# An encoder trunk on one core: order of the norm transitions and of the cross attention's head norms

## The reference, cut to what matters

```
h = rms_norm(x, mix_norm[l])
x = x + mixer(h) @ w_out          # layer 0: RWKV-7 and a gating MLP; layer 1: differential attention
# cross attention, 4 heads of 256, into 256 memory tokens
q = rms_norm((rms_norm(x, cross_norm[l]) @ wq).reshape(.., 4, 256), q_gain)
kv = rms_norm(mem, mem_norm) @ wkv
k = rms_norm(kv[..., :1024].reshape(.., 4, 256), k_gain);  v = kv[..., 1024:]
x = x + (softmax(q k^T / 16) v) @ wo
# gated MLP, width 2816
u = conv3(rms_norm(x, ffn_norm[l]) @ w_up)
x = x + (silu(gate) * val) @ w_down
```

## Time and profile before

| | |
|---|---|
| median of 3 runs | 1874.19 us (1871.98 to 1876.8) |
| the profiled execution's own time | 1874.89 us |
| its span, first to last instruction | 1873.1 us |
| PE busy with matmuls | 1759.9 us, 94% of the span |
| DVE, ACT, POOL busy | 989.2, 766.8, 100.6 us |
| mean granted TensorE clock | 0.984 of full speed |

### The profile page before, as it was taken

One profiled execution on the slowest core, in us unless ns is written; L12 is line 12 of the kernel. 1 busy time (PEld: TensorE's weight loads), 2 busy tenths in 40 slices (PEclk: granted clock), 3 DMA queues, 4 the chain that ended last, 5 costly groups with the idle time before them and its releaser, 6 DMA issues.

```text
span 1873.1 us, 31962 instructions
## 1 busy us (share of the span) xinstructions
PE 1759.9 (94%) x14153; PEld 1442.8 (77%) x14153; DVE 989.2 (53%) x1353; ACT 766.8 (41%) x1158; POOL 100.6 (5%) x79
## 2 busy tenths in 40 slices
PE   6997888889999999999998999999998999999999
PEld 5876777767778788888887887557777878888887
DVE  5477656467434456534644244994534356633652
ACT  4243444334644334413433234773554244422431
POOL 1001221000000000000000022000000000000000
PEclk9999999989999999999998999999999999999999
DMA  7210000033331222233212322002322213322221
GB/s 237 79 45 2 4 4 4 5 136 122 135 112 45 68 90 91 99 103 111 92 68 90 112 78 80 1 1 91 134 68 91 83 60 105 110 93 90 90 83 75
DMA packets 96452, 149.40 MB, mean 80 GB/s; under 512 B 3479, under 2 KB 50170, under 8 KB 96314
## 3 DMA queue, kind: packets, MB, share of 16 engines
q1 hardware_dynamic: 94727, 142.29, 22.6%
q0 software_dynamic: 1296, 4.95, 0.8%
q10 hardware_dynamic: 291, 0.12, 0.0%
HBM read 145.25 MB, written 2.10 MB: 79 GB/s over the span
## 4 chain that ended last, share of the span: by engine, by line
PE 79%; DVE 11%; ACT 5%; issue 3%; DMA 2%; POOL 1%; POOLq 0%; DVEq 0%; SPq 0%; ACTq 0%
PE PS L373 65%; DVE SS L1560 1%; PE PS L506 1%; PE PS L956 1%; DVE WLO L338 1%; ACT WHI L330 1%; PE PS L1349 1%; PE PS L1318 1%; PE PS L942 1%; PE PS L983 1%; PE PS L975 1%; PE PS L588 1%; DMA WRAW<-cross_wo 1%; DMA WRAW<-cross_wq 1%; DVE YQ L1287 1%
## 5 line engine op out<-in xcount | busy, mean ns | idle before, releaser
L338 DVE TENSOR_TENSOR WLO<-WRAW,WHI 128x2048 fp32r<-128x2048 f32 (+1 forms) x132 | 296.7, 2251 | 458.3 <-ACT WHI L330 458.3
L330 ACT ACTIVATE WHI<-WRAW 128x2048 fp32r<-128x2048 f32 (+1 forms) x132 | 248.1, 1880 | 471.1 <-PE PS L373 442.6
L373 PE MATMUL PS<-HIS,WHI 128*128 128x512 f32 x856 | 333.8, 390 | 1.5 <-DVE SM L1722 1.5
L373 PE MATMUL PS<-HIS,WLO 128*128 128x512 f32 x856 | 333.0, 389 | 0.0
L373 PE MATMUL PS<-LOS,WHI 128*128 128x512 f32 x856 | 333.0, 389 | 0.0
L373 PE MATMUL PS<-WHI,HIS 128*128 128x512 f32 x608 | 239.1, 393 | 7.3 <-DVE WLO L338 3.5
L373 PE MATMUL PS<-WLO,HIS 128*128 128x512 f32 x608 | 237.4, 391 | 0.0
L373 PE MATMUL PS<-WHI,LOS 128*128 128x512 f32 x608 | 237.3, 390 | 0.0
L373 PEld LDWEIGHTS PS<-HIS,WHI 128*128 128x128 f32 x856 | 160.7, 188 | 35.0 <-DVE SM L1722 1.7
L373 PEld LDWEIGHTS PS<-HIS,WLO 128*128 128x128 f32 x856 | 160.7, 188 | 33.6
L373 PEld LDWEIGHTS PS<-LOS,WHI 128*128 128x128 f32 x856 | 160.7, 188 | 33.4 <-issue 0.2
(11 more groups left out here) (280 smaller groups left out, 2467.1 us busy)
## 6 DMA issues: line engine op xcount, KB each, us to landing
WRAW<-ffn_w_up SPq DMA_DIRECT2D x88, 512.0 KB, 4.6
WRAW<-ffn_w_down SPq DMA_DIRECT2D x20, 1024.0 KB, 5.0
WRAW<-cross_wkv SPq DMA_DIRECT2D x16, 1024.0 KB, 5.0
WRAW<-diff_w_in SPq DMA_DIRECT2D x12, 1024.0 KB, 5.0
WRAW<-ab_w_in SPq DMA_DIRECT2D x10, 1024.0 KB, 5.3
WRAW<-cross_wq SPq DMA_DIRECT2D x8, 1024.0 KB, 5.0
WRAW<-cross_wo SPq DMA_DIRECT2D x8, 1024.0 KB, 5.1
X<-x SPq DMA_DIRECT2D x8, 512.0 KB, 7.2
```

The lines of the kernel that those rows point to most:

```text
L330: A.e.activation(part(WHI[i % 3], i), part(WRAW[i % 2], i), ACT.Copy).then_inc(S("w_hi"), 1)
L338: V.e.tensor_tensor(part(WLO[i % 3], i), part(WRAW[i % 2], i), part(WHI[i % 3], i).bitcast(F32), ALU.subtract).then_inc(S("w_lo"), 1)
L373: mm = e.matmul(o, l, r, start=(si == 0 and kk == 0 and q == 0), stop=(si == len(steps) - 1 and kk == nk - 1 and q == 2))
```

## The change

- A product whose operand comes from a norm waits for each block k before that block's first matmul, in tile b = 0, instead of for four blocks ahead of the slab.
- The squares of the three tile-wise norm transitions are taken by half rows: the first half's squares (and their DVE step, with the epsilon) stand in the evacuation of the first column half; the second half's squares are 512 wide, and the mean-square instruction adds the first half's.
- `norm_pe` for n1 uses all eight banks and does not wait from k = 4 on.
- kk's second column half uses banks 2 and 3 instead of 0 and 1. The bank waits are kept per bank instead of per base.
- Head norms go tile by tile: DVE's mean squares (4 columns), POOL's power (4 columns) and DVE's scaling stand in the evacuation of the second column half, the scaling one tile behind.
- The query transposes stand ahead of the tiles of slab kv1 instead of kv2 on PE, and ACT's evacuation of them ahead of its split of slab kv1 + 2 = kv3, by a new argument `ahead`.

```diff
@@ gemm_pe
-            if operand is not None and gi == 0:
-                e.wait_ge(*operand(kb + nk))
...
-                if si == 0 and banks_before[name, gi] is not None:
+                if si == 0 and banks_before[name, gi, b] is not None:
...
                     k = kb + kk
+                    if operand is not None and gi == 0 and b == 0:
+                        e.wait_ge(*operand(k + 1))
@@ gemm_side
             for i, _, _ in steps:
+                if ahead is not None:
+                    ahead(s)
                 split(E, i + 3 if limit is None else min(i + 3, limit))
@@ bank_base
+        if name.startswith("kk") and gi == 1:
+            return 2
@@ square_tile_act
-            if gi == 1:
-                A.e.wait_ge(*at(name, "ev", n + 1))
-                if b > 0:
-                    A.e.wait_ge(*at(tag, "sq", b))
-                A.e.activation(SQ[:, :], X[:, b, :], ACT.Square, accum_out=SM[:, b:b + 1]).then_inc(sem(tag, "sq"), 1)
+            half = slice(gi * 512, gi * 512 + 512)
+            A.e.wait_ge(*at(name, "ev", n + 1))
+            if n > 0:
+                A.e.wait_ge(*at(tag, "sq", n))
+            o = (12, 0)[gi] + b
+            A.e.activation(SQ[:, half], X[:, b, half], ACT.Square, accum_out=SM[:, o:o + 1]).then_inc(sem(tag, "sq"), 1)
@@ var_tile_dve and residual_and_norm_dve
+    def half_var_dve(V, tag, t):
+        V.e.wait_ge(*at(tag, "sq", t + 1))
+        V.mine(V.e.tensor_scalar(SM[:, 12 + t:13 + t], SM[:, 12 + t:13 + t], 1.0 / D, EPS, ALU.mult, ALU.add))
...
-        V.e.wait_ge(*at(tag, "sq", t + 1))
-        V.e.tensor_scalar(SM[:, 4 + t:5 + t], SM[:, t:t + 1], 1.0 / D, EPS, ALU.mult, ALU.add).then_inc(sem(tag, "var"), 1)
+        V.e.wait_ge(*at(tag, "sq", NT + t + 1))
+        V.e.tensor_scalar(SM[:, 4 + t:5 + t], SM[:, t:t + 1], 1.0 / D, SM[:, 12 + t:13 + t], ALU.mult, ALU.add)\
+            .then_inc(sem(tag, "var"), 1)
...
+            if gi == 0:
+                if b >= 1:
+                    half_var_dve(V, tag, b - 1)
+                if b == NT - 1:
+                    half_var_dve(V, tag, b)
+                    V.wait_mine()
@@ norm_pe
-            if k >= 4:
+            if k >= 4 and b0 is not None:
@@ head_norm_dve
-        V.e.wait_ge(*at(name, "ev", gemms[name][-1][2] + gemms[name][-1][1]))
-        group_var_dve(V, tag, nt, XD, 32 + o, 96 + o)
+        def evac(gi, b, banks):
+            if gi == 1:
+                e.wait_ge(*at(name, "ev", banks + 1))
+                s = 32 + o + b * n
+                e.tensor_scalar(SM[:, s + 64:s + 64 + n], SM[:, s:s + n], 1.0 / XD, EPS, ALU.mult, ALU.add)\
+                    .then_inc(sem(tag, "gvar"), 1)
+                if b > 0:
+                    scale(b - 1)
+                if b == nt - 1:
+                    scale(b)
@@ head_norm_pool
         for t in range(nt):
-            group_scale_dve(V, tag, tok, t, XD, 160 + o)
+            G.e.wait_ge(*at(tag, "gvar", t + 1))
+            s = 96 + o + t * n
+            G.e.tensor_tensor(SM[:, s + 64:s + 64 + n], SM[:, s:s + n], SM[:, 16:17].to_broadcast([P, n]), ALU.pow)\
+                .then_inc(sem(tag, "grstd"), 1)
@@ query_turn_pe
-            if (gi, si) == (1, 0):
+            if (gi, si) == (0, 1):
+                if b == 0:
+                    T.e.wait_ge(*at(f"xq{l}", "ev", 2 * NT))
@@ tensor_program and scalar_program
-                norm_pe(T, "n1", XN, NT, 4)
+                norm_pe(T, "n1", XN, NT, None)
...
             def query_turn(s):
-                if s == 2:
+                if s == 1:
...
-            gemm_side(A, f"kv{l}", split_hi, copy_out(A, f"kv{l}", to_tok(VMEM)), only=0)
-            gemm_side(A, f"kv{l}", split_hi, None, beside=query_turn, only=1)
+            gemm_side(A, f"kv{l}", split_hi, copy_out(A, f"kv{l}", to_tok(VMEM)), ahead=query_turn, only=0)
+            gemm_side(A, f"kv{l}", split_hi, None, only=1)
```

More of the change, by code:

```diff
@@ L378, in gemm_pe, with gemm_side @@
                 mm.then_inc(sem(name, "wused"), 1)
-    def gemm_side(E, name, split, evac, limit=None, beside=None, only=None):
+    def gemm_side(E, name, split, evac, limit=None, beside=None, only=None, ahead=None):
         s = 0
@@ L403, in bank_base, with norm_bank @@
             return 6
+        if name.startswith("kk") and gi == 1:
+            return 2
         return 4 if name.startswith("dn") or (name, gi) == ("ab", 1) else 0
-    banks_before, before = {}, {0: None, 4: None, 6: None}
+    banks_before, before = {}, [None] * 8
     for _name, _groups in gemms.items():
         for _gi, (_, _nb, _banks) in enumerate(_groups):
-            banks_before[_name, _gi] = before[bank_base(_name, _gi)]
-            before[bank_base(_name, _gi)] = (_name, _nb, _banks)
+            for _b in range(_nb):
+                _bank = bank_base(_name, _gi) + _b
+                banks_before[_name, _gi, _b] = before[_bank]
+                before[_bank] = (_name, _banks + _b + 1)
     def bank_free(name, gi, b):
-        other, nb, banks = banks_before[name, gi]
-        return at(other, "ev", banks + min(b, nb - 1) + 1)
+        other, n = banks_before[name, gi, b]
+        return at(other, "ev", n)
     hhi, hlo = (lambda k: HHI[k][:, :]), (lambda k: HLO[k][:, :])
+    def norm_bank(b0, k):
+        return k if b0 is None else b0 + k % 4
     def norm_act_front(A, tag, src, sq, nt, arrives=False, added=None):
@@ L435, in norm_act_back @@
             e.wait_ge(*at(tag, "tp", k + 1))
-            e.activation(hi(k)[:, 0:nt * P], PS[:, b0 + k % 4, 0:nt * P], ACT.Copy,
+            e.activation(hi(k)[:, 0:nt * P], PS[:, norm_bank(b0, k), 0:nt * P], ACT.Copy,
                          scale=gain(k)).then_inc(sem(tag, "hi"), 1)
@@ L454, in norm_dve_back @@
             e.wait_ge(*at(tag, "hi", k + 1))
-            e.scalar_tensor_tensor(lo(k)[:, 0:nt * P], PS[:, b0 + k % 4, 0:nt * P], gain(k),
+            e.scalar_tensor_tensor(lo(k)[:, 0:nt * P], PS[:, norm_bank(b0, k), 0:nt * P], gain(k),
                                    hi(k)[:, 0:nt * P].bitcast(F32), ALU.mult, ALU.subtract).then_inc(sem(tag, "lo"), 1)
@@ L486, in evac @@
             add(gi, b, n)
-            if gi == 1:
+            if gi == 0:
[4 more added lines that the diff above has]
+                    V.wait_mine()
+            else:
                 if b >= 1:
@@ L505, in norm_pe @@
                     e.wait_ge(*at(tag, "xn", t + 1))
-                mm = e.transpose(PS[:, b0 + k % 4, t * P:t * P + P], xn[:, t, k * P:k * P + P], ident)
+                mm = e.transpose(PS[:, norm_bank(b0, k), t * P:t * P + P], xn[:, t, k * P:k * P + P], ident)
             mm.then_inc(sem(tag, "tp"), 1)
@@ L559, in evac @@
             for q in range(2):
-                A.e.activation(SQX[:, 0:XD], PS[:, b, q * XD:q * XD + XD], ACT.Square,
+                A.e.activation(SQX[:, 0:XD], PS[:, bank_base(name, gi) + b, q * XD:q * XD + XD], ACT.Square,
                                accum_out=SM[:, sums + 4 * b + 2 * gi + q:sums + 4 * b + 2 * gi + q + 1])\
@@ L563, in evac, with scale, head_norm_pool @@
                 A.e.wait_ge(*at(name, "hsum", 2 * n + q + 1))
-            A.e.activation(dst(gi, b), PS[:, b, :], ACT.Copy).then_inc(sem(name, "ev"), 1)
+            A.e.activation(dst(gi, b), PS[:, bank_base(name, gi) + b, :], ACT.Copy).then_inc(sem(name, "ev"), 1)
         return evac
     def head_norm_dve(V, tag, name, tok, nt, o):
-        V.e.wait_ge(*at(name, "ev", gemms[name][-1][2] + gemms[name][-1][1]))
-        group_var_dve(V, tag, nt, XD, 32 + o, 96 + o)
+        e, n = V.e, D // XD
+        def scale(t):
+            e.wait_ge(*at(tag, "grstd", t + 1))
+            v = tok[:, t, :].rearrange("p (g w) -> p g w", w=XD)
+            e.tensor_tensor(v, v, SM[:, 160 + o + t * n:160 + o + t * n + n].unsqueeze(2).to_broadcast([P, n, XD]), ALU.mult)\
+                .then_inc(sem(tag, "gn"), 1)
+        def evac(gi, b, banks):
[8 more added lines that the diff above has]
+                    scale(b)
+        return evac
+    def head_norm_pool(G, tag, nt, o):
+        n = D // XD
         for t in range(nt):
-            group_scale_dve(V, tag, tok, t, XD, 160 + o)
+            G.e.wait_ge(*at(tag, "gvar", t + 1))
+            s = 96 + o + t * n
+            G.e.tensor_tensor(SM[:, s + 64:s + 64 + n], SM[:, s:s + n], SM[:, 16:17].to_broadcast([P, n]), ALU.pow)\
+                .then_inc(sem(tag, "grstd"), 1)
     def group_norm_pool(G, tag, nt, w, o=0):
@@ L1748, in norm_shares @@
         n = nt if by_tile else 1
-        shares(tag, "norm", sq=nt, var=n, rstd=n, xn=nt, tp=DC, hi=DC, lo=DC)
+        shares(tag, "norm", sq=2 * nt if by_tile else nt, var=n, rstd=n, xn=nt, tp=DC, hi=DC, lo=DC)
     def turn_shares(tag, nt):
-        n = DH if tag == "do" else 1
+        n = DH if tag == "do" else nt if tag[0] == "x" else 1
         shares(tag, "turn", gvar=n, grstd=n, gn=DH if tag == "do" else nt, ttp=DC, tev=DC, hi=DC if tag == "do" else 0)
@@ L1958, in vector_program @@
             if l == 1:
```

(8 more changed lines are left out.)

4 lines of the change are left out of this document (2 added, 2 removed).

## The result

The changed kernel takes 1856.82 us (median of 4, 1856.34 to 1859.2); the kernel before, with one more run beside it, 1873.62 us. The ratio is 0.9905, 95% interval 0.9892 to 0.9917: 16.8 us less, where 17.0 was forecast. The profiled execution took 1856.78 us, 18.1 less than the one of before.

What follows compares the result with a forecast made beforehand. PE carries 79% of the chain, so time is won at its waits. Terms 3.2 + 11.8 + 2.0 = 17.0 us take the profiled 1874.9 to 1857.9; that execution lay 0.7 above the median, so 1857.2 us, range 1852 to 1865.

Steps and rivals of the forecast that it cites:

- Keys and banks: Start of xq: PE no longer waits for ACT's evacuation of the keys; 1.6 us in each layer, 3.2 us.
- Queries: Cross attention, kv's first product to first logits: 25.7 us falls to 19.8, 5.9 in each layer, 11.8 us.
- the slack of 0.15: Cross attention: the queries' last scaling ends 0.15 us before PE turns to their transposes ahead of kv1.
- What is late next: Softmax weights behind ACT's later kv3 split: ready 1.3 us before PE needs them, so nothing lost; the tightest place.
- Rival 1: Softmax starts late: load, splits or evacuations take 3 to 4 us more, PE waits 2 to 3 per layer; 1862, 16%.
- Squares: Norm transitions, squares by half rows: 0.4 us each at nf0 and nf1, 1.2 at n1, together 2.0 us.
- Eight banks and waits for each k: Norm transitions: no gain, as PE's transposes are slow at half clock; at full clock n1 would win about 1.1 us.
- rival 2: Norm transitions' idle gaps: clock staying up gives up to 7 us more, 1850; staying down longer, 1861; 17%.
- Rivals 3 and 4: Nothing comes of the query part, 1869, 4%; or slower, as ACT's late kv3 split delays the softmax weights, 1879, 3%.

Runs made afterwards that it cites:

- e1: Kernel before with only kk's second half in banks 2 and 3 and bank waits kept per bank; 1867.97 us, ratio 0.9970.
- e2: Kernel before with only the query part: head norms tile by tile and query transposes at slab kv1; 1861.04 us, ratio 0.9933.
- e5: Kernel before with only the query transposes moved to slab kv1, head norms in one piece; 1874.32 us, ratio 1.0001.
- e6: Kernel before with only the head norms tile by tile, query transposes at kv2 as before; 1863.04 us, ratio 0.9938.
- e7: Changed kernel with four unused 1024-wide squares on ACT between query evacuation and kv3's split in each layer; 1869.52 us in one execution.
- e4: Kernel before with only the waits for each k and the eight banks of n1; 1872.33 us, ratio 0.9995.
- e11: Changed kernel with spare products on PE in the norm transitions' gaps, but n1 back on four banks; 1854.86 us, ratio 0.9897.
- e9: Changed kernel with spare products on PE in the gaps of the three norm transitions; 1851.39 us, ratio 0.9882.
- e12: As e10, but products wait once for each slab of four blocks, as in the kernel before; 1854.45 us, ratio 0.9885.
- e3: Kernel before with only the squares by half rows; 1870.15 us, ratio 0.9981.
- e8: Changed kernel with each tile's scaling directly behind its own power, so none runs beside a power; 1859.20 us in one execution.
- e10: As e9, with eight banks at nf0 and nf1 too; 1849.82 us, ratio 0.9870.

## Why the prediction was right

- **Keys and banks: 3.2 forecast, 3.5 in the trace of the change, 3.75 alone (e1).** The mechanism is as worked out; the term was read from the wait's row, 1.6 in each layer. A row's idle time begins where the last product's row ends, and a row is 0.39 us long where products follow every 0.227. A wait that goes away therefore gives back 0.16 more than its row says, and 1.58 + 0.16 = 1.74 is what e1 shows (1.77 and 1.75). The changed kernel has 1.69 and 1.55, for its nx transposes waited 0.28 and 0.36 for a low half, where the kernel before waited 0.21 and 0.17.
- **Queries: 11.8 forecast, 11.8 measured, 11.8 alone by e2's stages (12.1 by its medians).** 19.8 us of work were forecast between kv's first product and the logits, 19.88 are there. The power beside a scaling was taken at 2.0 and took 1.91; the slack of 0.15 was 0.10. What the forecast did not say is which half of the change brings it: e5 and e6 show that it is the norm tile by tile, through DVE's earlier split of kv2 and the earlier load of xo0. The move of the turn alone does nothing (e5), and on top of the norm it gives 0.2 in each layer.
- **What is late next: slack 1.3 forecast, 0.9 measured.** The first exponential was forecast 7.7 us after the logits (22.0 - 14.3) and came after 8.04. e7 bears the 0.9 out. Rival 1 named the right place; its condition, 3 to 4 us more than was counted, did not occur.
- **Squares: 2.0 forecast.** The gaps ahead of the last tile shrank by 0.47, 0.47 and, at n1, 1.28 (from 7.16 to 5.88 us after the last product): 2.2.
- **Eight banks and waits for each k: nothing forecast, nothing measured (e4).** The condition was the right one: at n1 the gain was put at 1.1 us if the clock were up, and e11 against e9 gives 1.13. Its make-up was not seen. The prediction says that the first slab's low halves have been waited for by the time the last transpose is issued. That holds with four banks only; with eight, and the clock up, the waits for each k carry 0.8 of the 1.13 (e12).
- **The clock, rival 2.** It was down in all three transitions, as forecast, but not for as long: 0.8 us of the 18.1 come from the lengths from the last tile's transposes to the first product (nf0 5.67 to 5.01, nf1 5.02 to 4.81, n1 5.81 to 5.90). The sum has no term for that. Nothing in the change itself makes the work of nf0 and nf1 shorter; the clock came back a little earlier, and whether the shorter gap brings that about is not shown (in e3, with the same gap, nf1 went the other way, to 5.79).
- **How much of the match is luck.** The profiled executions differ by 18.1, 1.1 over the forecast: 0.8 of the clock, 0.3 of the keys and 0.2 of the squares, less the 0.2 lost ahead of them. The medians differ by 16.8. A match to 0.2 us is closer than either can tell, with runs that spread over 2.9 and 4.8 us; the mechanism is borne out by the stages, not by that match.
- **Rivals 3 and 4** did not occur. 3 needed the queries' last tile to be late, and 0.1 us was left. e5 is its case, with the last scaling 4 us late, and there nothing came of the query part.

The power beside a 1.22 us scaling with two SBUF inputs took 1.91, and in e8, with nothing beside it, 1.01. The Trainium skill (SBUF — State Buffer, "Who interferes with whom") says that a DVE instruction with two SBUF inputs contends with a GpSimd instruction that reads SBUF. By that rule, the trace agrees: power and scaling overlap for 1.05 us, from 533.73 to 534.78, and the power is 0.90 longer.

**The better version.** e10 beats both kernels: 24.2 us less than the kernel before on the same chip, where the change alone had 16.8. Its three transitions take 22.8 us, against 29.1 in the change and 32.1 before.

## What to carry to other kernels

A wait is worth following to the transfer behind it: here PE waited for ACT, ACT for a load, the load for a buffer, and the buffer for a vector engine that stood in one long power and four scalings; cutting that first link into tiles gave nearly all of the query part's gain, and moving the work that had waited gave nothing without it. Where an engine's clock falls in gaps, finer waits and more banks bought nothing that could be measured, for the slow engine hides them; with the clock held up by spare work in the gaps, the two together were worth 1.1 us at each transition, and more banks without the finer waits only 0.4. When a wait is removed, add to its row the part of the last matmul's row that overlaps the next.

## What the runs showed of the hardware

- The granted clock over a gap of about 4 us went either way: behind nf0's gap it was 0.50 in the earlier trace rows and in the changed kernel, and 1.00 in e4 and in e7. With spare products in the gap it was 1.00 at all twelve transitions of e9 to e12. It also rose during plain transposes, with no product between, as in the kernel before at nf1:

```profile
1505.00:1508.00 3.00, 2.39 (x11) 2.39 (x12) 1.60 (x3) 1.55 (x3) 0.00 (x0) 0.52 0.00 0
...
1509.00:1510.00 1.00, 1.00 (x9) 0.70 (x7) 0.90 (x2) 1.00 (x3) 0.00 (x0) 1.00 0.00 0
```

- The first transposes of the memory tokens came at 443.5 (e2) to 450.0 us (e5) in kernels in which nothing ahead of them was changed, and at 446.5 (e9) to 452.7 us (e7) in those that share the changed kernel's code up to there. The spread arises in layer 0's recurrence: from its start at about 155 us to its end 247.7 us pass in e2 and 254.2 in e5. Of the stages behind, those without a wait agree to 0.05 us (xo takes 43.72 to 43.77 in all fourteen kernels); those with a gap, in which the clock may fall, do not. So a part that is worth 2 us is better priced from the stages of a trace than from the medians, and a stage with a gap in it from several traces.
